# Phase B cut into a K/V-and-query stage and an attention stage, with three tiles in flight instead of two

## The reference

```
layer A:  u = rms_norm(x) @ w_in;  xb, gate = halves of u
          xc = causal width-4 convolution of xb
          r = sigmoid(xc @ wa + ba); i = sigmoid(xc @ wx + bx)   (4 diagonal blocks)
          a = exp(8 r log_sigmoid(lam)); b = sqrt(1 - a^2) * i * xc
          h[t] = a[t] h[t-1] + b[t];     x = x + (h * silu(gate)) @ w_out
K/V:      k, v = rms_norm(x) @ w_kv;     k = rms_norm(k)         (2 heads of 64)
layer B:  q, gate = rms_norm(x) @ w_in_b;  q = rms_norm(q)/8     (16 heads of 64)
          o = softmax with a sink over 128 older keys + own chunk, ALiBi distances
          x = x + (o * silu(gate)) @ w_out_b
```

## Time and profile before

| | us |
|---|---|
| median of three runs (2010.48 to 2015.04) | 2013.48 |
| profiled execution | 2013.62 |
| its span on the slowest core (core 7) | 2012.6 |
| busy in the span: PE / DVE / ACT / POOL | 890.8 / 904.5 / 791.4 / 467.1 |
| spans of the eight cores | 2002.3 to 2012.6 |

### The profile page before, as it was taken

One profiled execution on the slowest core, in us unless ns is written; L12 is line 12 of the kernel. 1 busy time (PEld: TensorE's weight loads), 2 busy tenths in 40 slices (PEclk: granted clock), 3 DMA queues, 4 the chain that ended last, 5 costly groups with the idle time before them and its releaser, 6 DMA issues. The chain is left out here.

```text
span 2012.6 us, 24127 instructions; the slowest of 8 cores (2002.3 to 2012.6 us)
## 1 busy us (share of the span) xinstructions
PE 890.8 (44%) x8089; PEld 658.6 (33%) x8089; DVE 904.5 (45%) x1811; ACT 791.4 (39%) x1230; POOL 467.1 (23%) x422
## 2 busy tenths in 40 slices
PE   0212333343232554554645545545646546443543
PEld 0212233343222442443434424424424334241431
DVE  3265677777543334334343343353343433433331
ACT  2126366575333344344244333433343442433422
POOL 0040332333101222123122222222221231221211
PEclk9955665666656775766767766767667667666756
DMA  3432200000420000000000000000000000003200
GB/s 84 144 109 81 89 22 21 22 1 0 140 70 0 1 22 0 22 22 1 22 22 1 22 21 1 22 1 21 22 1 22 22 1 21 12 1 11 4 11 2
DMA packets 28210, 56.11 MB, mean 28 GB/s; under 512 B 11231, under 2 KB 15735, under 8 KB 28087
## 3 DMA queue, kind: packets, MB, share of 16 engines
q1 hardware_dynamic: 28087, 54.57, 9.7%
HBM read 45.93 MB, written 8.75 MB: 27 GB/s over the span
## 5 line engine op out<-in xcount | busy, mean ns | idle before, releaser
L75 POOL TENSOR_TENSOR BB<-TB,EAB 128x1024 bf16<-128x1024 f32 x68 | 144.5, 2125 | 526.8 <-ACT TB L75 492.4
L75 DVE SCALAR_TENSOR_TENSOR TA<-XB,PVT,TA 128x128 f32<-128x128 f32 x345 | 170.6, 495 | 32.4 <-DVE TA L75 0.9
L75 PE MATMUL PD<-VA,BB 128*128 128x65 bf16 x512 | 38.9, 242 | 226.8 <-POOL BB L75 214.8
L75 PE MATMUL PC<-WinB,BB 128*128 128x512 bf16 x272 | 104.6, 567 | 78.1 <-DVE BB L75 78.1
L75 ACT ACT_TABLE_LOAD x85 | 109.1, 1283 | 58.3 <-PE PC L75 16.9
L75 PE MATMUL PA<-BA,WinA 128*128 128x128 bf16 x1472 | 126.4, 262 | 10.3 <-ACT BA L75 10.3
L75 ACT ACTIVATE TB<-PC,MNEG 128x1024 f32<-128x1024 f32 x68 | 75.4, 1109 | 132.4 <-PE PC L75 128.2
L75 PEld LDWEIGHTS PA<-BA,WinA 128*128 128x128 bf16 x1472 | 120.2, 122 | 13.8 <-issue 12.0
L75 DVE SCALAR_TENSOR_TENSOR TA<-TA,PB 128x1024 f32<-128x1024 f32 x18 | 22.0, 1220 | 228.0 <-ACT TA L75 228.0
L75 PE MATMUL PT<-IDB,BB 128*128 128x128 bf16 x360 | 41.4, 285 | 155.1 <-DVE BB L75 82.3
L75 PEld LDWEIGHTS PD<-VA,BB 128*128 128x128 bf16 x512 | 31.4, 128 | 238.6 <-issue 238.6
(11 more groups left out here) (178 smaller groups left out, 2292.9 us busy)
## 6 DMA issues: line engine op xcount, KB each, us to landing
X<-xp SPq DMA_DIRECT2D x17, 512.0 KB, 3.3
TB<-w_in_b SPq DMA_DIRECT2D x16, 512.0 KB, 4.6
yp<-X SPq DMA_DIRECT2D x16, 512.0 KB, 2.7
X<-xpre SPq DMA_DIRECT2D x10, 512.0 KB, 3.7
TB<-w_in_a SPq DMA_DIRECT2D x8, 512.0 KB, 4.2
TA<-w_in_a SPq DMA_DIRECT2D x8, 512.0 KB, 3.8
TA<-w_out_a SPq DMA_DIRECT2D x8, 512.0 KB, 3.3
TA<-w_out_b SPq DMA_DIRECT2D x8, 512.0 KB, 3.3
```

What stands on the lines that cost most here:

```text
L75: return f(*a, **kw)
```

## The change

Phase B becomes two generators: `phaseB1` (norm, K/V, queries up to QN) and `phaseB2` (gate, score steps, output). A stage now emits B2 of tile i, B1 of tile i+1 and A of tile i+2. So that both can be open at once, K and V get a third slot, QN and the transposed x get two buffers each (the new ones in the memory of XB1, which the main part doesn't use), the queries go to PB, and layer A uses BS0P, that is PA for all its matmuls. The prefetch of the next main tile is dropped. In a score step the yield between the V matmuls and the DVE instructions goes, and the two large DVE instructions change their roles: SGB is first scaled by 0.5/denominator, then multiplied with PD. Two small constants move into other tiles.

```diff
+    IDF, bIDF = TA[5][0][:, 0:128], TA[5][1]
+    VOUT, bVOUT = CTMP[:, 0, :], bCTMP
+    XB1bf = XBS[1][0][:, :, :].rearrange("p c t -> p (c t)").bitcast(BF16)
+    QN2 = (XB1bf[:, 0:D], Buf("QN2"))
+    X1T2 = (XB1bf[:, D:2 * D], Buf("X1T2"))
+    QNR = [BB_[2], QN2]
+    X1TR = [BB_[1], X1T2]
...
-    def phaseB(tp):
+    def phaseB1(tp):
...
-        yield from rms_to_T(X1c, bX1c, SMB, bSMB, BB_[0], BB_[1])
+        yield from rms_to_T(X1c, bX1c, SMB, bSMB, BB_[0], tp["X1T"])
...
-                op("pe", [bX1T, bWinB], [bPC, bPC0, bPC1],
-                   lambda e, oc=oc, kc=kc: e.matmul(v3(PC)[:, oc, :], ...
+                op("pe", [bX1T, bWinB], [bPB],
+                   lambda e, oc=oc, kc=kc: e.matmul(v3(PB)[:, oc, :], ...
...
+        QN, bQN = tp["QN"]
+        op("dve", [bPB, bRQ], [bQN], lambda e: e.tensor_tensor(QN[:, :], PB[:, :], RQ[:, :], ALU.mult))
+        yield
+
+    def phaseB2(tp):
+        if tp["kvonly"]:
+            return
...
-            yield
             O3 = PD[:, 0:260].rearrange("p (j e) -> p j e", e=65)
...
-            op("dve", [bPD, bSMO], [bTMPO], ... TMPO = PD * SMO_[4:8], tensor_tensor
-            op("dve", [bTMPO, bSGB], [bOGb], ... OGb = TMPO * 0.5 * SGB, scalar_tensor_tensor
+            op("dve", [bSGB, bSMO], [bSGB], ... SGB = SGB * 0.5 * SMO_[4:8], scalar_tensor_tensor
+            op("dve", [bPD, bSGB], [bOGb], ... OGb = PD * SGB, tensor_tensor
...
-        cur = j % 2
-        prev = 1 - cur
+        cur = j % 3
+        prev = (j - 1) % 3
...
-            Hprev=HPREV, X1=X1[j % 3], Xbuf=X1[j % 3], carry=True, bs=BS0, ...
+            Hprev=HPREV, X1=X1[j % 3], Xbuf=X1[j % 3], carry=True, bs=BS0P, ...
+            QN=QNR[j % 2], X1T=X1TR[j % 2],
...
-    for j in range(len(tiles) - 1):
-        tiles[j]["prefetch"] = tiles[j + 1]
...
     run_streams([phaseA(tiles[0]), deferred_winb()])
+    gens = [phaseB1(tiles[0])]
+    if len(tiles) > 1:
+        gens.append(phaseA(tiles[1]))
+    run_streams(gens)
     for i in range(len(tiles)):
-        gens = [phaseB(tiles[i])]
+        gens = [phaseB2(tiles[i])]
         if i + 1 < len(tiles):
-            gens.append(phaseA(tiles[i + 1]))
+            gens.append(phaseB1(tiles[i + 1]))
+        if i + 2 < len(tiles):
+            gens.append(phaseA(tiles[i + 2]))
         run_streams(gens)
```

More of the change, by code:

```diff
@@ L253, in build @@
     WoutB, bWoutB = sb("WoutB", [128, NCH, D], BF16)
-    IDF, bIDF = sb("IDF", [128, 128], F32)
     IDB, bIDB = sb("IDB", [128, 128], BF16)
@@ L287, in build @@
     HC, bHC = sb("HC", [128, NCH], F32)
-    K2, bK2 = sb("K2", [128, 2, 2, 2, 128], BF16)
-    VA, bVA = sb("VA", [128, 2, 2, 65], BF16)
+    K2, bK2 = sb("K2", [128, 3, 2, 2, 128], BF16)
+    VA, bVA = sb("VA", [128, 3, 2, 65], BF16)
     K2S, bK2S = sb("K2S", [128, 2, 2, 2, 128], BF16)
@@ L292, in build @@
     KOUT, bKOUT = sb("KOUT", [128, 128], F32)
-    VOUT, bVOUT = sb("VOUT", [128, 128], F32)
     KD, bKD = sb("KD", [128, 2, 2, HD], BF16)
     bWinA2 = Buf("WinA_gate")
-    bK2s = [Buf("K2_0"), Buf("K2_1")]
-    bVAs = [Buf("VA_0"), Buf("VA_1")]
+    bK2s = [Buf("K2_0"), Buf("K2_1"), Buf("K2_2")]
+    bVAs = [Buf("VA_0"), Buf("VA_1"), Buf("VA_2")]
     bK2Ss = [Buf("K2S_0"), Buf("K2S_1")]
     bVASs = [Buf("VAS_0"), Buf("VAS_1")]
+    IDF, bIDF = TA[5][0][:, 0:128], TA[5][1]
[3 more added lines that the diff above has]
+    X1T2 = (XB1bf[:, D:2 * D], Buf("X1T2"))
+    XBS[1][1].parts = [QN2[1], X1T2[1]]
+    QNR = [BB_[2], QN2]
+    X1TR = [BB_[1], X1T2]
     PT0, bPT0 = ps("PT0", [128, D], BF16)
@@ L445, in build @@
     op("dve", [], [bHC], lambda e: e.memset(HC[:, :], 0.0))
-    op("dve", [], [bK2s[0], bK2s[1]], lambda e: e.memset(K2[:, :, :, :, :].rearrange("p a b c d -> p (a b c d)"), 0.0))
+    op("dve", [], bK2s, lambda e: e.memset(K2[:, :, :, :, :].rearrange("p a b c d -> p (a b c d)"), 0.0))
     op("dve", [], [bK2Ss[0], bK2Ss[1]], lambda e: e.memset(K2S[:, :, :, :, :].rearrange("p a b c d -> p (a b c d)"), 0.0))
@@ L703, in phaseB @@
         so = tp["state_out"]
-        yield from rms_to_T(X1c, bX1c, SMB, bSMB, BB_[0], BB_[1])
-        X1T3 = v3(BB_[1][0])
-        bX1T = BB_[1][1]
+        yield from rms_to_T(X1c, bX1c, SMB, bSMB, BB_[0], tp["X1T"])
+        X1T3 = v3(tp["X1T"][0])
+        bX1T = tp["X1T"][1]
         yield
@@ L744, in phaseB @@
             for kc in range(NCH):
-                op("pe", [bX1T, bWinB], [bPC, bPC0, bPC1],
-                   lambda e, oc=oc, kc=kc: e.matmul(v3(PC)[:, oc, :], WinB[:, kc, oc * 128:(oc + 1) * 128], X1T3[:, kc, :],
+                op("pe", [bX1T, bWinB], [bPB],
+                   lambda e, oc=oc, kc=kc: e.matmul(v3(PB)[:, oc, :], WinB[:, kc, oc * 128:(oc + 1) * 128], X1T3[:, kc, :],
                                                     start=(kc == 0), stop=(kc == NCH - 1)),
@@ L751, in phaseB @@
         SQ, bSQ = BB_[0]
-        op("act", [bPC], [bSQ], lambda e: e.activation(SQ[:, :], PC[:, :], AF.Square))
+        op("act", [bPB], [bSQ], lambda e: e.activation(SQ[:, :], PB[:, :], AF.Square))
         yield
@@ L762, in phaseB @@
         yield
-        QN, bQN = BB_[2]
-        op("dve", [bPC, bRQ], [bQN], lambda e: e.tensor_tensor(QN[:, :], PC[:, :], RQ[:, :], ALU.mult))
+        QN, bQN = tp["QN"]
+        op("dve", [bPB, bRQ], [bQN], lambda e: e.tensor_tensor(QN[:, :], PB[:, :], RQ[:, :], ALU.mult))
         yield
+    def phaseB2(tp):
+        nv = tp["nv"]
+        if tp["kvonly"]:
+            return
+        X1c, bX1c = tp["X1"]
+        K2t, bK2l, VAt, bVAl = tp["K2"], tp["bK2"], tp["VA"], tp["bVA"]
+        cur, prev = tp["cur"], tp["prev"]
+        X1T3 = v3(tp["X1T"][0])
+        bX1T = tp["X1T"][1]
+        QN, bQN = tp["QN"]
         for half in range(2):
@@ L811, in phaseB @@
                                                              VAt[:, cur, kvh, :], start=False, stop=True), inc=(j == 3))
-            yield
             O3 = PD[:, 0:260].rearrange("p (j e) -> p j e", e=65)
             h0 = kvh * 8 + hf * 4
+            sl = slice(step * 256, (step + 1) * 256)
             op("dve", [bPD, bSINKE], [bSMO],
@@ L818, in phaseB @@
             op("dve", [bSMO], [bSMO], lambda e, SMO_=SMO_: e.reciprocal(SMO_[:, 4:8], SMO_[:, 0:4]))
[L819 to L827, removed]
+            op("dve", [bSGB, bSMO], [bSGB],
+               lambda e, SMO_=SMO_, sl=sl: e.scalar_tensor_tensor(
+                   SGB[:, sl].rearrange("p (j d) -> p j d", j=4), SGB[:, sl].rearrange("p (j d) -> p j d", j=4), 0.5,
+                   SMO_[:, 4:8].unsqueeze(2).to_broadcast([n, 4, HD]), ALU.mult, ALU.mult))
+            op("dve", [bPD, bSGB], [bOGb],
+               lambda e, O3=O3, sl=sl: e.tensor_tensor(
+                   OGb[:, sl].rearrange("p (j d) -> p j d", j=4), O3[:, :, 0:64],
+                   SGB[:, sl].rearrange("p (j d) -> p j d", j=4), ALU.mult))
             yield
@@ L832, in phaseB @@
                inc=(kc == NCH - 1))
-        OGT, bOGT = BB_[1]
+        OGT, bOGT = tp["X1T"]
         op("act", [bPT0], [bOGT], lambda e: e.activation(OGT[:, :], PT0[:, :], AF.Copy))
@@ L863, in build @@
             nv=128, x_src=xp[j * 128:(j + 1) * 128, :], y_dst=(None if halo else yp[(j - 1) * 128:j * 128, :]),
-            Hprev=HPREV, X1=X1[j % 3], Xbuf=X1[j % 3], carry=True, bs=BS0, XBn=XBS[0], idx=NPRE + j, dep=None,
+            Hprev=HPREV, X1=X1[j % 3], Xbuf=X1[j % 3], carry=True, bs=BS0P, XBn=XBS[0], idx=NPRE + j, dep=None,
+            QN=QNR[j % 2], X1T=X1TR[j % 2],
             K2=K2, bK2=bK2s, VA=VA, bVA=bVAs, cur=cur, prev=prev, kmcol=(2 if halo else 0), hist_init=None,
@@ L875, in build @@
         Hprev=((lambda c: PVT[:, 88 + c:89 + c]), bPVT), X1=X1[(NTH + 1) % 3], Xbuf=X1[(NTH + 1) % 3], carry=False,
-        bs=BS0, XBn=XBS[0], idx=-1, dep=None,
+        bs=BS0P, XBn=XBS[0], idx=-1, dep=None, QN=QNR[(NTH + 1) % 2], X1T=X1TR[(NTH + 1) % 2],
         K2=K2S, bK2=bK2Ss, VA=VAS, bVA=bVASs, cur=1, prev=0, kmcol=1, hist_init=sample_hist,
```

## The result

The changed kernel takes 2173.41 us (median of 8 runs, 2170.81 to 2176.91), the kernel before 2014.94 beside it (8 runs): a ratio of 1.0787 [1.0774, 1.0801]. Predicted were 2038 us and a range of 1985 to 2085. The direction was right; the size was far off.

What follows compares the result with a forecast made beforehand. No engine but a chain per stage was taken as the bound, layer A's after the cut. Stages of 80.4 us and the rest summed to 1444.5 against 1419.8, +24.7 on 2013.6, making 2038 us; range 1985 to 2085.

Steps and rivals of the forecast that it cites:

- Order on the queues, B2 early, second part under load: Regular stage: planner's instruction order worked out; B2's addition near 48 us; convolution's 15 instructions averaging well over 500 ns.
- The first part of A: Layer A from stage start to the WGA matmuls: 49.0 us against 46.8 before, bounds 44.6 and 55.
- The copy to XB ends near 16.6: Early in layer A: this copy ends near 16.6 us from the stage's start.
- The 4.4 us lost to POOL: Layer A's convolution: DVE slows beside POOL, 0.7 lost per us over 6.3 us, so 4.4 us.
- The four DVE instructions keep their number and shapes ... taken as nothing: Fused score step: the missing yield shifts -0.5 to +1 us per stage, counted as nothing.
- The bound for WoutB ahead of WGA: Second part of A: 34 us if WoutB's 16 matmuls, 6.4 us after idle time, stand before WGA.
- The PSUM tile, 2.3 to 3.7: Layer A on one PSUM tile: WGX waits for tanh, gate matmuls for the XB copy; 2.3 to 3.7 us per stage.
- Second part, 31.4: Layer A from WGA matmuls to the next stage: 29.1+2.3 = 31.4 us, undisturbed by B2, against 31.5 before.
- one more than the three of before: ACT table loads: one more per stage for B2's tanh, 1.28 us each; 60 or more in fifteen stages instead of 46.
- The sample's stage, 86.4: Stage with the sample: 6 us above a regular 80.4; late tile clearing and loading lets B2 run ahead.
- Rival 1: Convolution gets ahead of B2's products: WGA at about 44.6, period 76, 1972 us; chance 0.28.
- Rival 3: Full collision: B2 meets the convolution in all four steps, WoutB ahead of WGA; period 84 or more, 2090 us up; chance 0.12.

Runs made afterwards that it cites:

- e4_small_products: Changed kernel with the score steps' POOL products cut from 1024 to 8 columns, a probe that computes something else: period 81.9 us.
- k1_hold_k: Changed kernel with only B2's score step 0 held until B1's K transposes are emitted: 4.5 us a stage less.
- f3_oldscore: Changed kernel with the score step's old pair of large DVE instructions and its yield: 1.83 us a stage less, stages of 85.2 to 89.0.
- e2_wgx_pb: Changed kernel with the main tiles' WGX matmuls back in PB: the period falls by 2.84 us.
- k2_h2_pa: h2_hold_mix_add with WGX's matmuls back in PA: period 75.54 us against 73.57.
- f4_before_pa: Kernel before with one edit, layer A of the main tiles using PA for all its matmuls: 2021.51 us against 2012.33.
- e1_two_deep: Changed kernel with B1 and B2 of a tile in one stream again, beside layer A of the next tile: period 84.5 us.
- f7_before_pa_qpb: Kernel before, two tiles deep, with layer A in PA alone and phase B's queries in PB: 2101.1 us.
- h2_hold_mix_add: Changed kernel with steps 0, 2, 3 and B2's addition held, WGX in PB, old DVE pair: 1943.18 us, ratio 0.9632 to the kernel before.
- g_hold2: Changed kernel with B2's score steps 2 and 3 held until layer A's convolution is emitted: 6.75 us a stage less.
- e3_hold0: Changed kernel with B2's score steps held, from the first on, until layer A's convolution is emitted: period 88.4 us.

## Why the prediction was wrong

- **Order on the queues, B2 early, second part under load: right.** Stages end with layer A, B2's addition is 32 us before their end, the mean of the fifteen is 512 ns.
- **"The first part of A", 49.0: the step that failed.** It measured 56.5. (1) "The copy to XB ends near 16.6" left out that product 0 runs beside B1's K chain: it ended at 19.8. e4_small_products puts 3.4 us a stage on this, k1_hold_k 2.6, with QN moved as well. (2) The 4.4 us lost to POOL were applied to the fifteen scalar_tensor_tensor only. They lost 2.4; the tensor_scalar lost 2.7, and the new scaling of SGB, which reads SBUF twice where the old pair first read PSUM, 2.2 in steps 2 and 3 (the old pair's second instruction is not spared either: 0.43 to 1.88 in f3_oldscore). That is 7.3, and e4_small_products shows that 3.6 of it go with the products; the rest is layer A's own POOL instructions. "The four DVE instructions keep their number and shapes ... taken as nothing" was the wrong half of the same slip. (3) The bound for WoutB ahead of WGA stood in the second part, and was not taken, because I had B2's addition at 48, so its matmuls over by 47; they ended at 56.7. It costs 2.7.
- **The PSUM tile, 2.3 to 3.7: right in size where nothing covers it** (e2_wgx_pb 2.8, k2_h2_pa 2.0), but f4_before_pa shows that it costs 0.2 in the order of before. Its size was right by the row; whether it is paid depends on who else is in the second part.
- **Second part, 31.4: 1.0 short,** in part for the extra table load. Fourteen stages have 56 loads, where I had one more than the three of before: four each, counted rightly and priced in the wrong place.
- **The sample's stage, 86.4: 99.9.** I took it that B2 running ahead would clear the way for it. The trace puts 7.3 us of the 13.5 at the stage's end. Layer A's addition is over at 2072.1, but the next stage's first instruction on ACT is queued behind a copy to CST, which waits for the store of the sample's convolution state. The copy to XB comes 10 us later than in a regular stage (28.9), and DVE's 36.7 us busy say that it collides here as well. No run takes this stage apart.

```profile
2070.88 1.22 DVE L75 TENSOR_TENSOR X<-X,PA 128x1024 f32<-128x1024 f32 x1 [5.86 <-PE PA L75]
2079.36 0.22 ACT L75 ACTIVATE CST<-TA 128x8 f32<-128x8 f32 x1 [22.90 <-DMA sconv<-CST]
```

- **Rival 1** (the convolution gets ahead, 76) came only in kernels with the holds. **Rival 3**, at 0.12, had the time (WGA at 52 or later, 84 or more, 2090 us and up) but not the way to it. Only its second half, WoutB ahead of WGA, was the case; three products beside the fifteen instructions are what e1_two_deep and f7_before_pa_qpb have (means of 715 and 735 ns), while the changed kernel has 512 and none. It was rated low because two of the four products are over before the convolution. They are, but the first of the two met K's chain. The range ended at a period of 83.5, so it left out not the end of rival 3, as the prediction says, but all of it.

Where the gain of a third tile went: cutting phase B does let layer A be the only chain, as h2_hold_mix_add shows (73.6 a stage). The way from 78.46 to 88.70 is walked by the runs step by step, one execution each: PA alone +0.24, the queries in PB +5.60, the new score steps and the missing prefetch, two tiles deep, +0.23, the third tile as ordered by the planner +4.17. The 5.60 are the collision on POOL and DVE inside the convolution. The 4.17 are not: between e1_two_deep and the changed kernel the convolution gets 1.8 us shorter, but starts 3.5 later, behind K's chain, and WoutB ahead of WGA adds 2.6.

## What to carry to other kernels

When a stream leaves the longest chain, ask which of its instructions will now fall beside the remaining chain's, and price each neighbour, the small ones ahead of the big stretch too. A planner that knows only durations and dependencies puts work as early as it can; freed buffers widen that freedom and can make a kernel slower. Three hold points in the emission, with WGX back in PB and the old pair of DVE instructions, turned 8% slower into 4% faster; g_hold2 shows that one hold alone gives 6.75 of the 15.1 us a stage, and e3_hold0 that one in the wrong place gives nothing. A wait read from a row is a price only where nothing fills it.

## What the runs showed of the hardware

- A 128x1024 product on POOL (2.12 us) stretches even one short DVE instruction to about its own length: KOUT 0.29 to 2.11, the scaling of SGB from 0.42 to 2.26. Five tensor_scalar beside one such product and two of layer A's POOL instructions go from 2.15 to 4.81. POOL itself is hardly slowed (2.12 to 2.28, once 2.40).
- The price of a wait on PE is at times more than the wait, as the granted clock behind it can be lower: the 16 xb matmuls behind 3.46 us took 1.69 (granted clock 0.60), behind 1.64 us in e4_small_products 1.05 (1.00). The wait alone doesn't say which: WGX's 16 took 1.86 behind 5.11 in the kernel after and behind 2.59 in f4_before_pa, but 1.05 and 1.36 behind 3.90 in two stages of k1_hold_k.
